# FFN gate/up as seven block products, a hidden layer that passes through DRAM, and a last stage of 512 columns

## The reference

```python
h = rmsnorm(x, ffn_norm_g)
x = x + (silu(h @ w_ffn_gate) * (h @ w_ffn_up)) @ w_ffn_down
gate = sigmoid(rmsnorm(x, ple_norm_g) @ w_ple_gate)
x = x + gate * (p @ w_ple_proj)
return rmsnorm(x, final_norm_g)
```

## Time and profile before

| what | value |
|---|---|
| profiled execution, first to last instruction (span) | 1394.8 us |
| three timed runs, median | 1396.05 us |
| PE busy | 1341.8 us, 96% of the span |
| DVE, ACT, POOL busy | 569.4, 367.3, 193.6 us |
| mean granted TensorE clock | 0.992 of full speed |
| DMA | 72.8 MB, 52 GB/s over the span |
| last matmul of the output projection issued | 532.90 us |
| FFN without a gap on PE from | 548.96 us |
| last down group begins | 1236.32 us |
| first unit of the last stage begins | 1267.49 us |

### The profile page before, as it was taken

How to read it: one execution, slowest core, us unless ns; L and a number is a source line. 1 busy time by engine, 2 the same in 40 slices (tenths; PEclk the granted TensorE clock), 3 DMA queues, 4 the chain that set the end, 5 groups by cost and what they waited for, 6 DMA issues and landing times.

```text
span 1394.8 us, 18527 instructions
## 1 busy us (share of the span) xinstructions
PE 1341.8 (96%) x6904; PEld 1148.5 (82%) x6904; DVE 569.4 (41%) x1053; ACT 367.3 (26%) x688; POOL 193.6 (14%) x351
## 2 busy tenths in 40 slices
PE   5999999979999999999999999999999999999997
PEld 5888788868887887888888888888888888879997
DVE  5634434475665133224233342415242425276113
ACT  5522122245654042221202111111111121134113
POOL 1334434440000031000000000000000000032215
PEclk9999999999999999999999999999999999999999
DMA  8211100010033010211111111111111111132002
GB/s 264 69 45 32 46 30 30 0 39 1 0 120 120 18 40 22 61 46 46 57 60 49 45 60 30 60 30 60 30 60 45 46 46 46 31 105 77 1 0 121
DMA packets 80289, 72.80 MB, mean 52 GB/s; under 512 B 2800, under 2 KB 70768, under 8 KB 80240
## 3 DMA queue, kind: packets, MB, share of 16 engines
q1 hardware_dynamic: 80096, 71.88, 16.5%
q10 hardware_dynamic: 144, 0.26, 0.1%
HBM read 67.94 MB, written 4.19 MB: 52 GB/s over the span
## 4 chain that ended last, share of the span: by engine, by line
PE 79%; issue 11%; POOL 6%; DVE 3%; ACT 1%; DMA 1%; POOLq 0%; SPq 0%; ACTq 0%; DVEq 0%
PE PS L1209 11%; PE PS L1210 11%; PE PS L1211 11%; PE PS L1247 5%; PE PS L1245 5%; PE PS L1246 5%; PE PS L191 3%; PE PS L856 3%; PE PS L193 3%; PE PS L192 3%; PE PS L872 2%; PE PS L1512 2%; PE PS L1514 2%; PE PS L1513 2%; POOL X L541 2%
## 5 line engine op out<-in xcount | busy, mean ns | idle before, releaser
L1209 PE MATMUL PS<-HTH,WF 128*128 128x512 f32 x704 | 274.1, 389 | 2.1 <-DVE HTL L235 2.1
L1211 PE MATMUL PS<-HTH,WF 128*128 128x512 f32 x704 | 273.9, 389 | 0.0
L1210 PE MATMUL PS<-HTL,WF 128*128 128x512 f32 x704 | 273.9, 389 | 0.0
L191 PE MATMUL PS<-WF,HTH 128*128 128x512 f32 (+1 forms) x448 | 178.1, 397 | 2.2 <-ACT X L316 1.5
L1099 DVE TENSOR_TENSOR X<-X,PS 128x512 f32<-128x512 f32 x192 | 127.8, 683 | 123.7 <-PE PS L193 64.4
L193 PE MATMUL PS<-WF,HTL 128*128 128x512 f32 (+1 forms) x448 | 174.4, 389 | 0.0
L1290 DVE TENSOR_TENSOR TMP<-TMP,PS 128x512 f32<-128x512 f32 x44 | 30.2, 687 | 352.6 <-ACT TMP L1277 352.6
L192 PE MATMUL PS<-WF,HTH 128*128 128x512 f32 (+1 forms) x448 | 174.1, 389 | 0.0
L1277 ACT ACTIVATE TMP<-PS 128x512 f32<-128x512 f32 x44 | 26.3, 598 | 520.7 <-PE PS L1211 520.7
L1209 PEld LDWEIGHTS PS<-HTH,WF 128*128 128x128 f32 x704 | 132.2, 188 | 29.6 <-issue 2.3
L1211 PEld LDWEIGHTS PS<-HTH,WF 128*128 128x128 f32 x704 | 132.2, 188 | 27.5
(11 more groups left out here) (154 smaller groups left out, 1876.3 us busy)
## 6 DMA issues: line engine op xcount, KB each, us to landing
RAW<-in_w_ffn_gate SPq DMA_DIRECT2D x22, 512.0 KB, 3.9
RAW<-in_w_ffn_up SPq DMA_DIRECT2D x22, 512.0 KB, 5.0
RAW<-in_w_ffn_down SPq DMA_DIRECT2D x22, 512.0 KB, 3.3
X<-in_x SPq DMA_DIRECT2D x16, 512.0 KB, 5.4
RAW<-in_w_in SPq DMA_DIRECT2D x32, 256.0 KB, 3.2
RAW<-in_w_o SPq DMA_DIRECT2D x16, 256.0 KB, 3.1
RAW<-in_w_ple_gate SPq DMA_DIRECT2D x8, 512.0 KB, 5.2
out_rows<-RAW SPq DMA_DIRECT2D x8, 512.0 KB, 2.6
```

Of the source, the lines that this page charges most:

```text
L191: nc.tensor.matmul(dst, HTH[:, k, tok], w_h, start=(k == 0), stop=False)
L1209: nc.tensor.matmul(dst, w_h, HTH[:, k, blk], start=(k == 0), stop=False)
L1210: nc.tensor.matmul(dst, w_h, HTL[:, k, blk], start=False, stop=False)
L1211: last = nc.tensor.matmul(dst, w_l, HTH[:, k, blk], start=False, stop=(k == K - 1))
```

## The change

**FFN gate/up.** The weights of one hidden block are seen as a 2x2 matrix of blocks: A11 and A12 are the gate's weights for the first and last four blocks of rows, A21 and A22 the up's. The activations are a 2x2 matrix too: B11 and B21 the two halves of rows for the first 512 tokens, B12 and B22 for the last 512. Strassen's scheme in Winograd's form makes the four results from seven products: S1 = A21+A22, S2 = S1-A11, S3 = A11-A21, S4 = A12-S2 with T1 = B12-B11, T2 = B22-T1, T3 = B22-B12, T4 = T2-B21. Each product is 12 matmuls of 512 columns. POOL makes the four sums of weights of each block (`sums`); ACT and DVE split all seven left sides (`weight_hi`, `weight_lo`). The T are made once, at the end of the output projection, tile pair by tile pair (order of tiles 0, 4, 1, 5, ...): T1 and T2 by DVE, T3 and T4 by POOL, which also rebuilds B11 and B21 as the sum of their parts (`far`).

Results share banks. A11*B11 is copied from bank x to bank a by ACT (`first_product`), S2*T2 is summed onto x, DVE adds S1*T1 (kept in `SUM5`) into the other bank (`f_u4`), S3*T3 is summed onto x, DVE adds again (`f_c22`), S4*B22 and A22*T4 finish.

**Hidden layer and down.** The hidden block (two halves of 512 tokens) is stored to a DRAM tensor `HID`. After all 22 blocks the eleven down groups run one behind the other. Each loads two rows of blocks of `HID` and two of `w_ffn_down` into the four raw slots, split by ACT and DVE (`down_hi`, `down_lo`).

**Last stage.** 16 units of 512 columns in place of 32 of 256, two pairs of banks in turn; the transposes of p stand at the head of the first eight units; POOL splits six pieces ahead of the norm factors, DVE the last four.

```diff
--- before.py
+++ after.py
...
+        PRODUCTS = {"A11": "B11", "A12": "B21", "S4": "B22", "A22": "T4", "S1": "T1", "S2": "T2", "S3": "T3"}
+        FIRST = ("A11", "A12", "S1", "S2", "S3", "S4", "A22")
+        LATER = ("A11", "S1", "S2", "A12", "S3", "S4", "A22")
...
+        def ffn_turn(e, i):
+            e.wait_ge(n_ffn.normed, i + 1)
+            if i >= 2 and i % 2 == 0:
+                e.wait_ge(f_b_lo, 3 * (i // 2) - 1)
+            if i >= 2 and i % 2 == 1:
+                e.wait_ge(f_t12, 2 * (i // 2))
+            turn_rows(n_ffn, i)
...
+                e.wait_ge(n_ffn.turned, i + 1)
+                e.wait_ge(f_raw_sum, 2 * p + 1)
+                if p:
+                    e.wait_ge(f_t34, 2 * p)
+                    e.wait_ge(f_t_lo12, 2 * p)
+                nc.vector.tensor_tensor(T_RAW[0], bank(2), R11, ALU.subtract).then_inc(f_t12, 1)
+                e.wait_ge(f_b_hi, 3 * p + 3)
+                nc.vector.tensor_tensor(pair_cols("B22", 1, p), as_k(bank(3)), pair_cols("B22", 0, p).bitcast(F32),
+                                        ALU.subtract).then_inc(f_b_lo, 1)
+                e.wait_ge(f_t12, 2 * p + 1)
+                nc.vector.tensor_tensor(T_RAW[1], bank(3), T_RAW[0], ALU.subtract).then_inc(f_t12, 1)
...
+            weight_lo(e, 0, "A11")
+            weight_lo(e, 0, "A12")
+            b_rest(T - 2)
+            rows_x(e, n_ffn, T - 1, ORD[T - 1], 48)
+            b_rest(T - 3)
+            t_rest(T - 3)
+            b_rest(T - 1)
+            weight_lo(e, 0, "S1")
+            t_rest(T - 1)
+            for name in ("S2", "S3", "S4", "A22"):
+                weight_lo(e, 0, name)
...
+                e.wait_ge(f_t12, 2 * p + 2)
+                if p:
+                    e.wait_ge(f_t_lo34, 2 * p)
+                nc.gpsimd.tensor_tensor(T_RAW[2], T_RAW[1], R11, ALU.subtract).then_inc(f_t34, 1)
+                e.wait_ge(f_raw_sum, 2 * p + 2)
+                nc.gpsimd.tensor_tensor(T_RAW[3], R21, T_RAW[1], ALU.subtract).then_inc(f_t34, 1)
+                for n in range(2):
+                    e.wait_ge(f_t_hi, 4 * p + 3 + n)
+                    nc.gpsimd.tensor_tensor(pair_cols(f"T{n + 3}", 1, p), as_k(T_RAW[2 + n]),
+                                            pair_cols(f"T{n + 3}", 0, p).bitcast(F32), ALU.subtract).then_inc(f_t_lo34, 1)
+            for i in range(T):
+                norm_rstd(e, n_ffn, i, 48)
+                if i == 4:
...
+                    sums(e, 0, (1, 2))
...
+                    far(i - 3)
+            for i in range(T - 3, T):
+                far(i)
+            e.wait_ge(n_ffn.normed, T)
+            sums(e, 0, (3, 4))
...
+                if j:
+                    e.wait_ge(f_w_lo, upto(j - 1, f"S{n}"))
+                    e.wait_ge(f_s, 4 * (j - 1) + 4)
+                if n == 1:
+                    nc.gpsimd.tensor_tensor(s1, u0, u1, ALU.add).then_inc(f_s, 1)
...
+        def weight_hi(e, j, name):
+
+            if name[0] == "S":
+                e.wait_ge(f_s, 4 * j + int(name[1]))
+            if j:
+                e.wait_ge(f_prod, upto(j - 1, name))
+            nc.scalar.copy(part(name, 0), part_raw(j, name)).then_inc(f_w_hi, 1)
+
+        def weight_lo(e, j, name):
+            e.wait_ge(f_w_hi, upto(j, name))
+            nc.vector.tensor_tensor(part(name, 1), part_raw(j, name), part(name, 0).bitcast(F32),
+                                    ALU.subtract).then_inc(f_w_lo, 1)
...
+                e.wait_ge(f_w_lo, 7 * (j + 1))
+                e.wait_ge(f_s, 4 * (j + 1))
+                if j + 2 < NB:
+                    sp_gate_up(e, j + 2)
+                else:
+                    sp_down(e, 0, (0, 1) if j == NB - 2 else (2, 3))
+                e.wait_ge(f_h1, j + 1)
+                e.dma_start(HID[j * P:(j + 1) * P, HALF:S], H1).then_inc(s_h1, 16)
+                e.wait_ge(f_h0, j + 1)
+                e.dma_start(HID[j * P:(j + 1) * P, 0:HALF], H0).then_inc(s_h0, 16)
+            for g in range(1, NG):
+                for n in range(4):
+                    e.wait_ge(d_lo, 4 * (g - 1) + n + 1)
+                    sp_down(e, g, (n,))
...
+            def strassen(name, dst, first):
+                e.wait_ge(f_w_lo, upto(j, name))
...
+                    nc.tensor.matmul(dst, w_h, m_h, start=(first and k == 0), stop=False, skip_group_check=True)
+                    nc.tensor.matmul(dst, w_h, m_l, start=False, stop=False, skip_group_check=True)
+                    last = nc.tensor.matmul(dst, w_l, m_h, start=False, stop=(k == 3), skip_group_check=True)
+                last.then_inc(f_prod, 1)
...
+                    strassen(name, x, True)
+                    if j == 0:
+                        ffn_turn(e, T - 1)
...
+                if name == "S2":
+                    if j == 0:
+                        e.wait_ge(f_t_lo12, 8)
+                    e.wait_ge(f_dup, j + 1)
+                    strassen(name, x, False)
...
+                if name == "S3":
+                    if j == 0:
+                        e.wait_ge(f_t_lo34, 7)
+                    e.wait_ge(f_u4, j + 1)
+                    strassen(name, x, False)
...
+                    e.wait_ge(f_c22, j + 1)
+                    strassen(name, x, False)
+
+        def first_product(e, j):
+            e.wait_ge(f_prod, upto(j, "A11"))
+            nc.scalar.copy(bank(bank_a(j)), bank(bank_x(j))).then_inc(f_dup, 1)
...
+            if j:
+                first_product(e, j)
+            if more:
+                weight_hi(e, j + 1, "A11")
...
+            nc.scalar.copy(SUM5, y).then_inc(f_p5, 1)
+            if more:
+                weight_hi(e, j + 1, "S1")
+                weight_hi(e, j + 1, "S2")
...
+            if more:
+                weight_lo(e, j + 1, "A11")
+                weight_lo(e, j + 1, "S1")
+            e.wait_ge(f_p5, j + 1)
+            e.wait_ge(f_prod, upto(j, "S2"))
+            nc.vector.tensor_tensor(y, SUM5, x, ALU.add).then_inc(f_u4, 1)
+            if more:
+                weight_lo(e, j + 1, "S2")
+                weight_lo(e, j + 1, "A12")
+            e.wait_ge(f_prod, upto(j, "S3"))
+            e.wait_ge(f_u4, j + 1)
+            nc.vector.tensor_tensor(SUM5, SUM5, x, ALU.add).then_inc(f_c22, 1)
...
+            hidden_0(j)
...
+        def down_lo(e, g, n):
+            e.wait_ge(d_hi, 4 * g + n + 1)
+            nc.vector.tensor_tensor(down_part(g, n, 1), raw(n), down_part(g, n, 0).bitcast(F32),
+                                    ALU.subtract).then_inc(d_lo, 1)
...
-            e.wait_ge(o_added, 2 * T)
-            pe_gu(e, 0)
...
+            for j in range(NB):
+                dve_block(e, j)
+            for n in range(4):
+                down_lo(e, 0, n)
...
+            for g in range(NG - 1):
+                for n in range(16):
+                    add_down(e, g, n)
+                    if n % 4 == 1:
+                        down_lo(e, g + 1, n // 4)
...
+            def p_high(t):
+                e.wait_ge(p_turned, t + 1)
+                if t == 0:
+                    e.wait_ge(f_down, 16 * NG)
+                nc.scalar.copy(p_part(t, 0), p_bank(t)).then_inc(p_hi, 1)
+
+            def sigmoid(u):
+                e.wait_ge(g_done, u + 1)
+                if u >= 2:
+                    e.wait_ge(g_added, u - 1)
+                nc.scalar.activation(SIG[u % 2], bank(4 + 2 * (u % 2)), ACT.Sigmoid).then_inc(g_sig, 1)
...
+            for u in range(2 * T):
+                half, t = u // T, u % T
+                tok = slice(t * P, t * P + P)
+                gate, emb = bank(4 + 2 * (u % 2)), bank(5 + 2 * (u % 2))
+                if u >= 2:
+                    e.wait_ge(g_mul, u - 1)
+                if half == 0:
+                    for k in range(2):
+                        last = nc.tensor.transpose(PS[:, 5 + 2 * (u % 2), k * P:k * P + P], PIN[:, t, k * P:k * P + P], ident)
+                    last.then_inc(p_turned, 1)
+                    e.wait_ge(n_ple.lo, 2 * t + 2)
...
+                    e.wait_ge(e_lo, 2 + 4 * half + 2 * kh + 2)
...
+                if half == 0:
+                    e.wait_ge(p_lo, t + 1)
...
+                last.then_inc(g_done, 1)
+                if u < 2:
+                    ple_turn(e, T - 2 + u)
...
```

More of the change, by code:

```diff
@@ new lines, in as_k, with b_half, moving @@
+        def as_k(x):
+            return x.rearrange("p (k n) -> p k n", k=4)
+        T_FAR = [[WF[:, 8192 + 4096 * n + 2048 * y:10240 + 4096 * n + 2048 * y].rearrange("p (k n) -> p k n", k=4)
+                  for y in range(2)] for n in range(3)]
+        def b_half(y, rows, late):
+            return (HTL if y else HTH)[:, 4 * rows:4 * rows + 4, late * HALF:late * HALF + HALF]
+        B_HALF = {"B11": (0, 0), "B21": (1, 0), "B22": (1, 1), "T1": (0, 1)}
+        def moving(name, y):
+            if name in B_HALF:
+                return b_half(y, *B_HALF[name])
+            return T_FAR[int(name[1]) - 2][y]
@@ new lines, in block_order, with upto, part, raw_gu @@
+        def block_order(j):
```

(51 more changed lines are left out.)

728 lines of the change are left out of this document (383 added, 345 removed).

## The result

The changed kernel takes 1373.78 us (median of 4 runs, 1373.04 to 1376.93) against 1395.93 of the kernel before: a ratio of 0.9848, 95% interval 0.9834 to 0.9862, or 22 us less. Forecast were 1369.7 us and 26 less. The profiled run is the slowest of the four, 1376.93, with a span of 1375.1 us against 1394.8.

The account below looks back on a forecast made before the run. Bound: PE's number of matmuls. The terms sum to -31.35 us, with +5 for the clock -26.35, against the 1394.8 us span: 1368.4, in the runs 1369.7 us; range 1356 to 1386.

Parts of the forecast that it names:

- steps 1, 3, 5: Products: 264 matmuls fewer, -59.8 us; blocks 1 to 21: hand-offs covered, 0; down stage: p's transposes leave, -1.75.
- Rival (a): Slower than before: hand-offs come late in every block, at 0.6 us late each about 1409 us; chance 0.06.
- step 2: Head of the FFN, block 0: PE waits four times for other engines, POOL's sums at 1.29 us; +23.9 us.
- low bounds (POOL at 0.74) and the high one (2.40): Block 0's end by POOL's time per sum: 39.5 us at 0.74, 40.3 without exclusion, 75.9 at 2.40.
- steps 4, 6, 7: Hand-over to down: first output waits, +5.5 us; last down group: first turn waits, +2.6; last stage, unit 2 waiting: -0.9.
- step 8: Tail after the last matmul: shorter POOL add, earlier factor, wider sigmoid and multiply; -0.9 us.
- step 9: Half clock behind some of PE's new long gaps, two places taken: +5 us, between 0 and 12.
- its 8 us: Clock term if each of the long gaps brought the throttled clock, as the Trainium skill has it: some 8 us.
- the sum without the clock: All terms of the whole kernel except the clock's +5: -31.35 us.
- (b): Dear head: POOL at 1.6 us, half clock at every gap, fourth piece 3.5 later; some 1376 to 1387 us; chance 0.27.
- (c): Cheap head: no exclusion (-7.6) and no fall of the clock (-5); some 1355 to 1364 us; chance 0.18.
- (d): Scratch's round trip binds down, each group waiting for its rows; 5 us late a group gives 1420 us; chance 0.02.

Follow-up runs that it names:

- experiment 8: Changed kernel with DVE's add u4 made six times in place of once in blocks 1 to 21: 1431.69 us (2 runs), 58 more.
- experiment 1: Changed kernel with extra matmuls, results unread, in five of PE's gaps (output not the reference's): 1368.58 us against 1373.78.
- experiment 3: Changed kernel with ACT copying raw B11 and B21 out of PSUM and POOL's eight rebuilding sums gone: 1370.61 us against 1373.78.
- Experiment 4: Changed kernel with DVE's add u4 in block 0 ahead of the rests of A22 and block 1's A11 and S1: 1368.36 us.
- Experiments 5 to 7: Each against changed kernel: first down splits inside last block, 1370.26 us; sigmoid 0 ahead of last tile's parts, 1370.60; two of six splits between norm factors, 1370.06.
- experiment 2: Changed kernel with the third pair's T3 and T4 high parts ahead of the A11*B11 copy on ACT in block 0: 1371.22 us.

## Why the prediction was right, point by point

**Products, blocks, down groups** (steps 1, 3, 5): right to a tenth of a microsecond. Rival (a) was far from its turning point: experiment 8 shows 1.71 us of slack for the 1.8 that I gave.

**Head** (step 2): up to S1 the mechanism and the price of POOL hold, and with the gaps filled (experiment 1) the times do too: A11 12.0, S1 26.6, S3 40.6, block 1 48.8 behind the mark, for a forecast of 12.4, 25.8, 39.75 and 47.9. At S3 this is in part luck. The chain is the one that I worked out: POOL's last sum, DVE's rests, u4; experiment 3 moves the sum and S3 by the same 5.1. But the sum ends sooner (34.7 in the changed kernel, 32.3 with the gaps filled, for 37.1), and from its end to S3 it is 8 us, for which I had 2.65: my order left out the rests of block 1's A11 and S1 ahead of u4, and took every rest there at 0.68, although POOL goes on with block 1's sums beside them. The two errors nearly cancel. Experiment 4 moves those two rests and A22's behind u4. The low bounds (POOL at 0.74) and the high one (2.40) are out.

**Hand-over, last group, unit 2** (steps 4, 6, 7): 5.6 for 5.5; 5.3 idle for 6.7, as the fourth piece landed in 3.8 us, not 5; 3.8 for 3.75. Experiments 5 to 7 remove each alone.

**Tail** (step 8): this step failed, though it is small. I had a factor come 0.9 sooner; it takes 1.08 us in both kernels, beside a row of the norm on DVE. The last add is 0.44 shorter, as forecast, and the wider sigmoid and multiply take 0.49 more. Tail 10.2 for 10.1 before.

**Clock** (step 9): the term that was mis-sized. I priced the places in block 0 rightly and then took two of them, 5 us, expecting the fall behind some of the gaps only; no row said which. It came behind all six. In the profile it is 5.7 in block 0 (A11 and S3, for which I had 2.7 each; S1's and S2's is hidden in the wait for S3, as worked out; 0.9 of the 5.7 stays with the gaps filled), and, left out of my 5, 2.8 in the first down group, 1.6 at unit 2 and about 1.8 in the last group (3.6 us at 0.50). These 11.9 less the earlier mark and the quicker landing, with the tail, are nearly the table's 11.7. Filled gaps gave back 5 to 9 of it. The sentence beside that term, by which the lower clock is the default that activity releases (the Trainium skill, "TensorE: Matmul & The Clock Gate", "Part 1: The HAM clock gate"), agrees with every one of the six, and its 8 us were nearer; by the medians the kernel is 9.1 above the sum without the clock. How A11's slow product gets on the path I had not told: ACT copies it ahead of high parts that POOL needs (experiment 2).

Of the rivals, (b) in its clock alone came true, half clock at every gap; POOL's price and the landing were not dear. (c) falls with both of its parts, (d) with the unbroken down groups.

## What to carry to other kernels

When a change removes matmuls, look for the places where PE will wait for other engines, and price each twice: the idle time, and the half clock behind it. Call the second hidden only after following who waits for the slow product. Then look into the order of the engine that ends the wait: five of the six gaps (S1, S3, the hand-over, the first turn, unit 2) were long because of operations that stood ahead of the one that mattered, and were shortened by moving them.

## What of the hardware was not expected

- DVE and POOL beside each other, both from SBUF, take 1.68 us a pair, DVE stretched from 0.68 to 1.75 and POOL from 1.29 to 1.71. That is more than either alone and less than one behind the other (1.97).
- A wait of 1.94 us once a block, between stretches of dense work, brought the half clock in 7 of 20 blocks; gaps of 0.91 and 1.38 us ahead of S3, in the kernels with u4 first, left the clock at 1.00 (569 to 577 us in the first, 563.8 to 573 in the second).

```profile
563.79 0.47 PE L1399 MATMUL PS<-WF 128*128 128x512 f32 x1 [1.38 <-issue]
```
